# Two attention loops of a three-layer network on one core: ScalarE moved a block behind VectorE, side products spread over a head's four blocks, queries scaled ahead of time, the last output put between the products of the output projection

## The reference

```
for layer in (0, 1):
    x = x + 0.5 * swiglu(rms_norm(x), gate, up, down)      # hidden width 2816
    x = x + mixer(rms_norm(x))    # layer 0: causal pooling + causal attention (8 heads of 96,
                                  #          values of 64); layer 1: gated convolution
    x = x + 0.5 * swiglu(rms_norm(x), gate, up, down)
x = x + 0.5 * swiglu(rms_norm(x), ...)                     # hidden width 2752
x = x + concat(fourier_mixer, gqa_attention) @ w_out       # 8 query heads, 2 key heads, of 64
x = x + 0.5 * swiglu(rms_norm(x), ...)                     # hidden width 2752
return rms_norm(x)
```

## Time and profile before

| | |
|---|---|
| time, median of 3 runs | 2774.48 us (2773.96 to 2775.02) |
| the profiled execution: time / span | 2773.52 us / 2771.7 us |
| TensorE busy | 2719.8 us, 12528 matmuls |
| VectorE, ScalarE, GpSimd busy | 1333.7, 904.2, 135.4 us |
| idle of TensorE, whole span | 51.9 us |

### The profile page before, as it was taken

How to read it: one execution, slowest core, us unless ns; L and a number is a source line. 1 busy time by engine, 2 the same in 40 slices (tenths; PEclk the granted TensorE clock), 3 DMA queues, 4 the chain that set the end, 5 groups by cost and what they waited for, 6 DMA issues and landing times.

```text
span 2771.7 us, 31299 instructions
## 1 busy us (share of the span) xinstructions
PE 2719.8 (98%) x12528; PEld 2251.3 (81%) x12528; DVE 1333.7 (48%) x1909; ACT 904.2 (33%) x1288; POOL 135.4 (5%) x132
## 2 busy tenths in 40 slices
PE   8999999999999999999999999999999998999998
PEld 7888878888888888888888888888878877888786
DVE  5444358654443444434554444344443467644433
ACT  4232226542222332322223232222232336422221
POOL 0000005300000000000000000000000124000000
PEclk9999999999999999999999999999999999999999
DMA  4332332023322333233323333333323220233222
GB/s 156 100 94 92 97 88 78 24 84 104 101 94 91 102 94 99 92 99 92 106 92 94 101 95 95 97 97 99 92 84 100 81 88 24 61 106 100 85 91 71
DMA packets 282161, 252.29 MB, mean 91 GB/s; under 512 B 8353, under 2 KB 278817, under 8 KB 282017
## 3 DMA queue, kind: packets, MB, share of 16 engines
q1 hardware_dynamic: 282016, 250.29, 29.5%
HBM read 248.16 MB, written 2.10 MB: 90 GB/s over the span
## 4 chain that ended last, share of the span: by engine, by line
PE 81%; issue 13%; DVE 4%; ACT 2%; DMA 0%; POOLq 0%; POOL 0%; SPq 0%; DVEq 0%; ACTq 0%
PE bank L384 27%; PE bank L385 27%; PE bank L386 27%; DVE wl L1153 0%; DVE g_mx L1262 0%; PE bank L473 0%; DVE a_mx L1262 0%; DVE g_RB L1162 0%; PE bank L437 0%; PE bank L426 0%; ACT wh L789 0%; ACT g_P L873 0%; DVE X L1162 0%; DVE a_nb L1169 0%; DVE a_KT L1165 0%
## 5 line engine op out<-in xcount | busy, mean ns | idle before, releaser
L1153 DVE TENSOR_TENSOR wl<-raw,wh 128x1024 fp32r<-128x1024 f32 (+4 forms) x496 | 571.5, 1166 | 951.8 <-ACT wh L789 951.3
L384 PE MATMUL bank<-Xh,wl 128*128 128x512 f32 x2544 | 996.2, 392 | 11.1 <-DVE wl L1153 8.6
L386 PE MATMUL bank<-Xh,wh 128*128 128x512 f32 x2544 | 991.0, 390 | 0.0
L385 PE MATMUL bank<-Xl,wh 128*128 128x512 f32 x2544 | 990.9, 390 | 0.0
L789 ACT ACTIVATE wh<-raw 128x1024 fp32r<-128x1024 f32 (+4 forms) x496 | 492.0, 1007 | 977.0 <-PE bank L386 971.8
L384 PEld LDWEIGHTS bank<-Xh,wl 128*128 128x128 f32 x2544 | 475.8, 187 | 114.7 <-issue 10.5
L385 PEld LDWEIGHTS bank<-Xl,wh 128*128 128x128 f32 x2544 | 475.9, 187 | 102.8 <-issue 1.9
L386 PEld LDWEIGHTS bank<-Xh,wh 128*128 128x128 f32 x2544 | 475.8, 187 | 102.2
L384 PE MATMUL bank<-Hh,wl 128*128 128x512 f32 x1056 | 412.8, 391 | 0.0
L385 PE MATMUL bank<-Hl,wh 128*128 128x512 f32 x1056 | 410.9, 389 | 0.0
L386 PE MATMUL bank<-Hh,wh 128*128 128x512 f32 x1056 | 410.9, 389 | 0.0
(11 more groups left out here) (274 smaller groups left out, 1557.8 us busy)
## 6 DMA issues: line engine op xcount, KB each, us to landing
raw<-in_ffn_w_gate SPq DMA_DIRECT2D x128, 512.0 KB, 3.6
raw<-in_ffn_w_up SPq DMA_DIRECT2D x128, 512.0 KB, 3.8
raw<-in_ffn_w_down SPq DMA_DIRECT2D x114, 512.0 KB, 3.4
raw<-in_c_w_in SPq DMA_DIRECT2D x24, 512.0 KB, 3.7
raw<-in_w_in SPq DMA_DIRECT2D x10, 512.0 KB, 3.8
raw<-in_a_w_in SPq DMA_DIRECT2D x8, 512.0 KB, 3.7
raw<-in_a_w_out SPq DMA_DIRECT2D x8, 512.0 KB, 3.4
raw<-in_c_w_out SPq DMA_DIRECT2D x8, 512.0 KB, 3.4
```

The lines of the kernel that those rows point to most:

```text
L384: e.matmul(o, ll, rh, start=start, stop=False)
L385: e.matmul(o, lh, rl, start=False, stop=False)
L386: i = e.matmul(o, lh, rh, start=False, stop=stop)
L1153: e.tensor_tensor(lo, src, hi.bitcast(F), ALU.subtract).then_inc(wlo.up(("w", n)), 1)
```

## The change

1. **ScalarE and `invert` a block later.** `start(k)` does `exponentials(k - 1)` and `invert(k - 2)`; a score bank is given back one block later. ScalarE and VectorE convert queries and keys a block later than before.
2. **Side products spread.** `first_half` is done in two pieces of six matmuls, at k % 4 = 0 and 2, `output` part 0 at k % 4 = 3 and part 1 at k % 4 = 1. `put` is an iteration later.
3. **mB's queries are scaled** by GpSimd before they are transposed (eight operations of 128x512), so that `bias` and the exponential's scale fall away; the other head's queries and the `mixed` products move from ahead of the attention into its opening.
4. **The end.** `mixer_out` on TensorE becomes `second_half`: three quarters of the products of two tiles, `output(7, 1)`, three quarters of the next two, then the rest.
5. **`spread`** takes two float32r matmuls (a high and a low part of `diag`) for the float32 one; VectorE makes both parts.
6. **Hidden width 2752** ends in two tiles of 96 rows, not in 128 and 64.

```diff
@@ chunks
-        full = (top - k) // 128
+        full, rest = divmod(top - k, 128)
+        nk = full + (rest > 0)
+        if rest:
+            full -= 1
...
-            parts.append((rest, full, 1, w[k + full * 128:top, n0:n1].rearrange("(k p) n -> p k n", k=1)))
-        got.append((parts, n, full + (rest > 0)))
+        if rest:
+            parts.append((64 + rest // 2, full, 2, w[k + full * 128:top, n0:n1].rearrange("(k p) n -> p k n", k=2)))
+        got.append((parts, n, nk))
@@ Mixer, BankRing
-                return [((k - when) // 4, part) for part, when in enumerate((2, 5))
+                return [((k - when) // 4, part) for part, when in enumerate((3, 5))
                         if 0 <= k - when < 32 and (k - when) % 4 == 0]
+            def put_at(self, k):
+                return (k - 6) // 4 if k >= 6 and (k - 6) % 4 == 0 else None
...
+            def leave(self, *late):
+                self.free_banks.sort(key=lambda b: b in late)
@@ stats
-                    e.matmul(bank[:, :], ones[:, :], diag[:, :], start=True, stop=True).then_inc(mm.up(("rb", s)), 1)
+                    e.matmul(bank[:, :], onesR[:, :], diag[:, 0, :], start=True, stop=False)
+                    e.matmul(bank[:, :], onesR[:, :], diag[:, 1, :], start=False, stop=True).then_inc(mm.up(("rb", s)), 1)
@@ tensor_program, attention
-                    if k < 32:
-                        free(("score", s, k))
+                    if 1 <= k <= 32:
+                        free(("score", s, k - 1))
...
-                for k in range(36):
-                    if k < 32:
-                        turn_block(k)
+                for k in range(32):
+                    turn_block(k)
                     start(k + m.ahead)
+                    t = m.early_at(k, 0)
+                    if t is not None:
+                        first_half(s, t, (0, 1))
+                    t = m.early_at(k, 2)
+                    if t is not None:
+                        first_half(s, t, (2, 3))
                     for h, part in m.out_at(k):
                         output(h, part)
...
+                ring[0].leave(4, 5)
+                second_half(s, 0, (0, 1, 2))
+                output(7, 1)
+                second_half(s, 1, (0, 1, 2))
+                free(("out", s, 7))
+                ring[0].leave(4, 5)
+                for pair in range(2):
+                    second_half(s, pair, (3,))
+                for pair in range(2, 4):
+                    second_half(s, pair, range(4))
@@ tensor_program, mixer_fnet
-                    if which == 0 and 4 <= h < 8:
+                    if which == 0 and 2 <= h < 8:
...
-                turn_queries(4, 2)
-                turn_queries(5, 3)
...
                 def later():
+                    n, h, l, _ = chunk()
+                    for g in range(4):
+                        name = ("mixed", s, g)
+                        bank = take(ring[0].take(name), name)
...
+                        mm3(bank[:, :], h[:, g, :], l[:, g, :], gRB[:, g, :], gRB[:, 4 + g, :], True, True, name,
+                            *([("used", n)] if g == 3 else []))
+                        yield
+                    for g in range(4):
+                        ring[0].free(("mixed", s, g))
+                        yield
                     first_half(s, 0)
@@ scalar_program, attention
-                    if k < 32:
-                        exponentials(k)
+                    if 0 <= k - 1 < 32:
+                        exponentials(k - 1)
                     next(fill, None)
-                    if 0 <= k - 1 < 32:
-                        normalise(k - 1)
+                    if 0 <= k - 2 < 32:
+                        normalise(k - 2)
...
                     if k < 32:
                         turned_high(k)
+                    prepare(k + m.ahead + 3)
                     start(k + m.ahead)
@@ vector_program, norm and attention
-                tt(diag[:, :].rearrange("p (t q) -> p t q", t=4), bc(ident, 1, [128, 4, 128]),
-                   bc(r4[s % 2][:, :], 2, [128, 4, 128]), ALU.mult, ("diag", s))
+                ts(r4h[:, :], r4[s % 2][:, :], 1.0, None, ALU.mult, None)
+                for i, part in enumerate((r4h, r4l)):
+                    w.wait_ge(dve, HERE)
+                    tt(diag[:, i, :].rearrange("p (t q) -> p t q", t=4), bc(ident, 1, [128, 4, 128]),
+                       bc(part[:, :].bitcast(F), 2, [128, 4, 128]), ALU.mult, ("diag", s))
+                    if i == 0:
+                        tt(r4l[:, :], r4[s % 2][:, :], r4h[:, :].bitcast(F), ALU.subtract)
...
-                    if 0 <= k - 1 < 32:
-                        invert(k - 1)
-                    if k < 32:
+                    if 0 <= k - 2 < 32:
+                        invert(k - 2)
+                    if k < 32 and m.causal:
                         bias(k)
...
-                    prepare(k + m.ahead + 4)
-                    t = m.early_at(k, m.fill[0])
+                    prepare(k + m.ahead + 3)
+                    t = m.early_at(k, 0)
@@ vector_program, mixer_fnet, ahead of the folding
                 ts(gr8[:, :], r1[:, :], 0.125, None, ALU.mult, None)
+                w.wait_ge(pool, ("rq", s))
+                w.wait_ge(dve, HERE)
+                tt(gsc[:, :, :], grq[:, :, :], bc(gr8[:, :], 2, [128, 4, 8]), ALU.mult, ("sc", s))
@@ gpsimd_program, mixer_fnet
                 inverse_root(grq[:, :, :], gvq[:, :, :], [4, 8], ("rq", s), ("vq", s))
+                w.wait_ge(dve, ("sc", s))
+                w.wait_ge(pool, HERE)
+                for h in range(8):
+                    q = gqtm[:, :, h].rearrange("p t a b -> p t (a b)")
+                    tt(q, q, bc(gsc[:, :, h], 2, [128, 4, 128]), ALU.mult, ("scaled", s, h))
```

169 lines of the change are left out of this document (85 added, 84 removed).

## The result

The changed kernel takes 2762.98 us (median of 5, 2759.89 to 2765.83) where the kernel before takes 2774.48 (median of 5). That is 11.5 us faster by the medians, less than half of the 26.1 that I forecast, and at the upper edge of the range. The ratio is 0.9955, 95% interval 0.9944 to 0.9967, which times 2774.5 is 12.5 us; the change is small but clear of the noise.

What follows compares the result with a forecast made beforehand. TensorE was taken as the bound, with time to regain where chain latency stops it in the two attentions. Terms -8.5, -3.0, -6.8, -3.7 and -4.1 sum to -26.1 us: median 2748.4, range 2738 to 2763.

Steps and rivals of the forecast that it cites:

- Second attention, opening and middle: Second attention: scores during `seq` conversion gain 4.2 us in the opening; fewer TensorE stops gain 8.5, middle and end.
- the close pair: Second attention's bank order: a queries' bank, converted a block later, is wanted a block after its transpose; 1.0 us kept.
- Causal attention up to the last output: Causal attention: -2.2 in the opening, -1.4 in the middle, -3.2 at the end, -6.8 us in all.
- What follows the last output: Second attention's end: 18 products of `second_half`, 4.1 us, cover a chain of two conversions of 0.6 to 0.7 each.
- Stage 8's lead-in: Before the second attention: VectorE's wait for GpSimd's power delays a weight split, stop 0.6, bound 1.3; +1.2 us together.
- GpSimd holds VectorE: Rival: GpSimd's eight products make VectorE wait, folding in stage 8 is late: +4, about 2753; 0.06 at its upper edge.
- `spread`: Nine stages with products behind them gain 0.41 us each from two float32r matmuls; very end 0: -3.7.
- 96 rows: Five down-projections in two stages lose the passage into 64 rows and back, 0.41 us each: -4.1.
- opening limits: Rival: VectorE-bound, the causal attention gives nothing and the other half of its 11.5: -13.6, 2761; chance 0.16.
- slower: Rival: at the close pair TensorE waits 2.3 us in 12 to 13 heads: +29 against 26, about 2778; chance 0.03.

Runs made afterwards that it cites:

- adds first: Changed kernel with VectorE's residual adds of a pair of output tiles ahead of the pair's Xl work, at both attentions' ends: 0.9931. Same on the kernel before: 0.9999.
- all of it undone: Changed kernel with lag, later output and laid-out products undone, banks returned as before, all else kept: 0.9977 to the kernel before.
- two of the runs: Changed kernel with the output a block sooner: 1.0006; changed kernel with the first half of the output matrix's products in one piece: 1.0003.
- the scaling undone: Changed kernel with GpSimd's scaling of the second attention's queries undone, bias and scale given to the exponential as before: 0.9944.
- the other orders mended: Changed kernel with adds first and keys ahead of the split; scaling undone gives 0.9907, scaling kept but VectorE's `g_rq` wait moved behind the folding 0.9896.
- keys ahead: Changed kernel with conversions of keys and first queries ahead of the second weight split in stage 8, on ScalarE and VectorE: 0.9940.
- the fastest kernel: Changed kernel with three orders changed, plus VectorE's causal opening reordered (second keys between query tiles, weight split later): 0.9889, median 2744.14 us.

## Why the prediction was wrong

By its own steps, in us of the profiled execution:

- **Second attention, opening and middle** (forecast -4.2 and -8.5): right in size, and too small if anything, though not by the parts that I had named (below), so partly by luck. Up to the last value product it gained 14.1, and 17.2 once the stop on `g_QS` was away (98.30 us). The close pair of banks, for which I kept 1.0, cost nothing.
- **Causal attention up to the last output** (forecast -6.8, of which the end -3.2): -4.7. The idle time at 455 to 548 fell to 7.7, as forecast, and the opening stayed VectorE's (21.48 of 25 us).
- **What follows the last output: the step that failed.** I wrote that "the end is covered by the 18 products of `second_half`" and counted the stops ahead of the output alone. I did not ask what those products had covered where they stood before. They had kept TensorE busy while VectorE and ScalarE took eight residual tiles through add, `Xh`, `Xl`, square and sum. With 78 products behind the output in place of 96, that chain is the longer one: +5.1 in stage 2 (3.2 of stop and 30 x 0.06 = 1.8 of clock) and +2.8 in stage 8 (stops of 0.73 and 1.50 among it). That is 7.9 of the 12.5 us by which the sum was short. The run with the adds first returned both to a tenth of a us; the same order on the kernel before was worth nothing.
- **Stage 8's lead-in** (forecast +1.2): +3.5, +3.9 without the gain of `spread`. I had the mechanism: a stop of 0.57 at the late split where I had 0.6, and one of 1.24 where my bound had 1.3, 1.8 in all. The term that the sum lacked is the slow clock behind such stops, 2.1 here. I had taken 1.6 of it as a gain in the causal attention and put it at nothing for every new stop. In this profile it was small: in nine others with the same matmuls and the same 2.1 us of idle time the lead-in took 59.69 to 61.89 us, at clocks of 0.96 down to 0.92. The rival "GpSimd holds VectorE" had the size, a loss of 4, but by luck: it put it all down to late folding. The traces bear out the rule of the Trainium skill (SBUF — State Buffer, Who interferes with whom): operations with two inputs in SBUF went from 0.42 to 1.27 us, and one with a bank as an input was not slowed.
- **The 3.0 us stop on `g_QS`**: not in the forecast. `mixed` moved into the attention, and the first scores moved up; the weight split that stands ahead of the keys' conversion on ScalarE had been harmless as long as `mixed` came first. I followed the four programs for that stretch and missed that this `use(2)` waits for the end of the `seq` products.
- **`spread`** (forecast -3.7): -0.45 or -0.46 in each of the five stages that show it bare, but the first factor stood 7.26 us behind its `sums`, not 6.50, and the very end took 0.1 more: 8 x -0.45 + 0.3 + 0.1 = -3.2. **96 rows** (forecast -4.1): 1.95 - 0.45 = 1.5 in stage 7 and the same in stage 9, -3.0. The down-projection of a stage took 1.75 us less, 0.35 a passage, not 0.41; about 0.3 is lost in `gate` and `up`, whose last pair of tiles now goes at 0.2319 us a start in place of 0.2290. By the rule of the Trainium skill (TensorE: Matmul & The Clock Gate, LDWEIGHTS) that only columns count, nothing would have been gained by that alone; the 1.5 us of each stage do not bear that out.

The sum: 7.2 short in stage 2, 4.1 in stage 8, 1.6 in the small edits, less the 0.4 by which the first `sums` came sooner: 12.5 in all, which is 26.1 less 13.6.

The rival "opening limits" had 13.6 and 2761, nearly what was measured, and this is luck. It had the attentions gain 5.8 and nothing lost around them; they gained 18.8, and 11.4 went at places that it did not name.

Of the reasons that I gave for the gain, one was over-valued. I laid the middle's gain on the interleaving (ScalarE free sooner, the output a block later). With all of it undone more than half of the attentions' 18.8 us is still there in the one profile; I had not seen how much the bias gone from VectorE and the moved products do for the same stops. And the rival "slower" had a real mechanism: one block's difference in the ring puts a stop of 1.2 to 2.0 us into four or five of an attention's eight heads and costs the whole gain, as two of the runs did. The change steers clear of it; my reading of the bank order by hand found the one pair that mattered, but did not show that it was harmless.

What stays open: why the same program, in the same stretch, is granted a different clock from run to run (below). How the 8.8 us of the second attention divide between the moved products and the missing bias was not measured; the scaling undone leaves it at 103.93 us, or 101.40 for 98.30 with the other orders mended, which speaks for 2.5 to 3.1 by the scaling.

## What to carry to other kernels

Work that is moved from B to A to cover a wait at A was covering something at B: list the other engines' chains that run beside it there, and compare their length with what is left. In a loop whose buffers come from a ring, write out which buffer each take gets before and after a change of order, and when its last reader is done; a part tried alone can look worthless or vital by its place in the ring only. A new stop of 3 us is to be priced with the slow clock that can follow it. And when a consumer moves up in time, look at every wait that stands ahead of its producer in that engine's queue, weight splits first.

## What the runs showed of the hardware

- **A stop can cost more than its length.** The 3.2 us stop ahead of stage 3 came with a clock of 0.94 over 550 to 580 in the three profiles that have it between 563 and 569 (the changed kernel, the scaling undone, keys ahead), and with adds first the clock was 1.00 in all four. Matmuls of 512 columns started 0.43 us apart from 1.3 us behind it, for 3 us, where 0.23 is normal: the 1.2 GHz level. In all the runs ten stretches behind a last output have such a stop, of 3.11 to 3.17 us, and their clock was 0.90 to 0.95 in nine and 1.00 in one. It is no fixed price: the second attention of the kernel before was idle for 17.0 us at a clock of 1.00, and the same instructions in another run (adds first, on the kernel before) for 14.9 at 0.95, which took 1.6 us longer.
- **The granted clock is not the same for the same program.** At 460 to 500 us, where the changed kernel and five of the experiments have the same instructions and the same stop of 1.9 to 2.0 us, the clock was 1.00 once, 0.96 twice, 0.91 twice and 0.87 once. The attention up to the last value product took 122.57, 124.04 and 124.14, 125.34 and 125.43, and 127.02 us with it. Two of the six, keys ahead of the split and then adds first:

```profile
460.00:500.00 40.00, 36.94 (x259) 33.44 (x259) 35.82 (x121) 26.93 (x74) 25.45 (x30) 1.00 0.17 54
...
460.00:500.00 40.00, 37.14 (x242) 33.79 (x241) 34.31 (x114) 25.35 (x70) 25.14 (x30) 0.91 0.12 40
```

  The changed kernel's five times lie 6 us apart, at a mean granted clock of 0.994 to 0.995 over the whole run; the four of the fastest kernel lie 0.7 apart, all at 0.998.
- **GpSimd beside VectorE nearly doubles the time of VectorE's work**: twelve operations of the folding took 9.4 us for 5.0 while GpSimd products of 128 x 512 ran. It goes the other way too: GpSimd's first two products took 1.97 and 2.03 us beside VectorE's weight splits, the next four 1.23 each.
